# Norms of the branches: squares summed on four output strips, inverse roots spread back by products on four row strips

## The reference

```
def head_norm(o, g, center):
    of = o.astype(jnp.float32)
    if center:
        of = of - jnp.mean(of, axis=-1, keepdims=True)
    y = of * lax.rsqrt(jnp.mean(of * of, axis=-1, keepdims=True) + EPS) * g.astype(jnp.float32)
...
    br_conv = jax.nn.silu(layernorm(conv + w['conv_b'], w['conv_ln_g'], w['conv_ln_b']))
    br_ret = jax.nn.silu(r_g) * head_norm(r_o, w['ret_gn'], center=True)
    br_gla = jax.nn.silu(g_r) * head_norm(g_o, w['gla_gn'], center=False)
    br_diff = head_norm(d_o, w['diff_subln'], center=False) * (1.0 - lam_init)
    gate = jax.nn.sigmoid(gates.reshape(B, L, N_BRANCH, D_MODEL))
    merged = jnp.einsum('blnc,ncd,blnd->bld', branches, w['w_branch'], gate)
    h = h + merged @ w['w_out']
```

## Time and profile before

| | |
|---|---|
| time, median of 3 runs | 2790.89 us (2789.33 to 2792.15) |
| span of the profiled execution | 2789.1 us |
| PE busy | 2767.2 us, 99% |
| DVE busy | 1986.8 us, 71% |
| ACT busy | 1206.8 us, 43% |
| norms of the branches, layer 0 | 838.15 to 869.78 us, with two gate tiles and a late gate tile |

### The profile page before, as it was taken

The page is one execution under the profiler, slowest core; times in us unless marked ns, Lnnn a source line. Parts: engine busy times, 40 slices in busy tenths (PEclk is TensorE's granted clock), DMA queues, the critical chain, the costliest instruction groups (busy, mean ns, idle before and its releaser), DMA issues.

```text
span 2789.1 us, 57776 instructions
## 1 busy us (share of the span) xinstructions
PE 2767.2 (99%) x21828; PEld 2687.1 (96%) x21828; DVE 1986.8 (71%) x3589; ACT 1206.8 (43%) x2160; POOL 128.2 (5%) x234
## 2 busy tenths in 40 slices
PE   8999999999999999999999999999999999999999
PEld 7999999998899999999999999999888999999999
DVE  8889534478667688887488895344787676899952
ACT  6445323435435254445254453234354343544521
POOL 0000001230000000000000000012300000000000
PEclk9999999999999999999999999999999999999999
DMA  4222326463234312223212223255733343122233
GB/s 138 91 95 98 108 75 198 155 202 131 98 117 172 140 64 91 90 90 114 91 67 92 90 98 106 68 198 163 214 118 121 108 178 130 61 92 103 98 106 103
DMA packets 104815, 325.92 MB, mean 117 GB/s; under 512 B 15055, under 2 KB 31855, under 8 KB 103104
## 3 DMA queue, kind: packets, MB, share of 16 engines
q1 hardware_dynamic: 91728, 280.67, 29.2%
q0 software_dynamic: 12912, 42.86, 4.8%
HBM read 291.45 MB, written 30.94 MB: 116 GB/s over the span
## 4 chain that ended last, share of the span: by engine, by line
PE 98%; DVE 1%; ACT 1%; issue 0%; DMA 0%; DVEq 0%; ACTq 0%; POOLq 0%
PE ps L1420 52%; PE ps L1449 35%; PE ps L1626 3%; PE ps L1432 1%; PE ps L1695 1%; PE ps L1911 1%; PE ps L1747 1%; PE ps L1728 1%; PE ps L1775 0%; PE ps L1795 0%; PE ps L1677 0%; PE ps L1737 0%; PE ps L1851 0%; PE ps L1934 0%; PE ps L1777 0%
## 5 line engine op out<-in xcount | busy, mean ns | idle before, releaser
L2063 DVE TENSOR_TENSOR w_lo<-w_raw,w_hi 128x1024 fp32r<-128x1024 f32 x240 | 292.7, 1224 | 353.0 <-ACT w_hi L814 349.4
L1449 PE MATMUL ps<-x_more,w_hi 128*128 128x296 f32 (+1 forms) x2112 | 456.8, 298 | 1.2 <-DVE x_more L2927 0.8
L1449 PE MATMUL ps<-x_hi,w_hi 128*128 128x296 f32 (+1 forms) x1408 | 420.0, 298 | 1.2 <-DVE w_lo L2101 1.2
L1449 PE MATMUL ps<-x_hi,w_lo 128*128 128x296 f32 (+1 forms) x1408 | 420.4, 299 | 0.0
L1449 PE MATMUL ps<-x_lo,w_hi 128*128 128x296 f32 (+1 forms) x1408 | 420.4, 299 | 0.0
L814 ACT ACTIVATE w_hi<-w_raw 128x1024 fp32r<-128x1024 f32 x224 | 234.9, 1053 | 407.2 <-PE ps L1420 240.1
L1420 PE MATMUL ps<-x_hi,w_hi 128*128 128x296 f32 (+1 forms) x1600 | 362.4, 308 | 3.8 <-ACT hT L1162 3.8
L2101 DVE TENSOR_TENSOR w_lo<-w_raw,w_hi 128x512 fp32r<-128x512 f32 x440 | 296.6, 690 | 88.4 <-ACT w_hi L862 85.8
L1449 PEld LDWEIGHTS ps<-x_more,w_hi 128*128 128x128 f32 x2112 | 351.0, 188 | 2.4 <-issue 1.3
L1420 PE MATMUL ps<-x_hi,w_lo 128*128 128x296 f32 (+1 forms) x1600 | 347.3, 299 | 0.0
L1420 PE MATMUL ps<-x_lo,w_hi 128*128 128x296 f32 (+1 forms) x1600 | 347.2, 298 | 0.0
(11 more groups left out here) (378 smaller groups left out, 4926.9 us busy)
## 6 DMA issues: line engine op xcount, KB each, us to landing
w_raw<-wstream SPq DMA_DIRECT2D x420, 512.0 KB, 3.6
kpage<-cache_k SPq DMA_DIRECT2D x128, 128.0 KB, 3.1
vpage<-cache_v POOLq DMA_DIRECT2D x128, 128.0 KB, 3.8
gate_rows<-hT SPq DMA_DIRECT2D x48, 296.0 KB, 2.3
d_sg<-gate_rows SPq DMA_DIRECT2D x16, 888.0 KB, 5.3
h_rows<-hT SPq DMA_DIRECT2D x2, 2368.0 KB, 9.5
hT<-h_rows SPq DMA_DIRECT2D x2, 2368.0 KB, 8.7
hT<-h_in SPq DMA_DIRECT2D x4, 592.0 KB, 8.3
```

Source lines behind the costliest of these rows:

```text
L1449: mm = pe.matmul(ps[:, bank, 0:span()], wp[:, k, :], xp, start=new and k == 0 and n == 0, stop=k == KH - 1 and n == 2, skip_group_check=True)
L2063: v.tensor_tensor(w_lo[:, slot, :, :], w_raw[:, slot, :, :], w_hi[:, slot, :, :].bitcast(F32), ALU.subtract).then_inc(weights_low, 1)
```

## The change

The squares of a tile are no longer summed with a 128x128 matrix of ones. A tile is cut into four strips of 148 columns (`strip()`), and each strip is multiplied with 32 columns of ones, so that its sums land on 32 rows of PSUM: strip r on rows 32r to 32r+31 of the same bank and columns (`strip_sums`, L1450 of the changed kernel). What took 592 columns on all rows takes 148. The sums of four norms fit in two banks, so one logarithm and one exponential over 128 x 592 do for four norms, and a second group (two logarithms, one exponential over 128 x 444) for the other three. The inverse roots go back to all 128 rows by products with a fourth matrix of ones, `ones[:, 3, :]`, from 32 rows each: strip r into its own bank (`spread`, L1456). VectorE's `normed` (L2857) reads them from PSUM, four banks at once.

The orders are changed with this. The first four sums stand ahead of the means. Gate tile 22 is cut in two halves: one in front of the mean over the conv tiles, one behind the first spread. The semaphore `hn_summed` becomes `hn_spread`. Three waits are new on TensorE: for two norms done (`hn_normed`, 2) ahead of the second spread, for four ahead of the third, and for all seven ahead of the first branch product. The matrix of ones grows from 192 to 256 KB.

```diff
-        ones = keep("ones", [P, 3, P])
+        ones = keep("ones", [P, 4, P])
...
+        HEAD_NORMS = (od_tiles[0:1], od_tiles[1:2], gla_tiles[0:1], gla_tiles[1:2], ret_tiles[0:1], ret_tiles[1:2], conv_tiles)
+        FIRST_NORMS = 4
+
+        def sum_at(i):
+
+            return i % FIRST_NORMS // 2, i % 2 * strip()
+
+        FIRST_SPREAD, LAST_SPREAD = (2, 3, 4, 5), (0, 1, 2, 3)
...
                 for i in range(4):
-                    square(i, HEAD_NORMS[i][2][0][0])
+                    square(i, HEAD_NORMS[i][0][0])
                 gate_out(l, 21)
-                for i in range(4):
-                    root(i)
-                for i in range(4):
-                    inverse(i)
+                root(FIRST_NORMS, 64, split_cols(hn_root[:, 0, :]), pair(0))
+                inverse(1, 0, 4)
                 for i, tile in enumerate((2, 3, 0, 1)):
                     act.wait_ge(hn_centered, i + 1)
                     square(4 + i, branch_tiles[tile])
                 gate_activated(l, 22)
-                for i in range(4, 7):
-                    act.wait_ge(hn_normed, i - 3)
-                    root(i)
-                for i in range(4, 7):
-                    inverse(i)
+                root(6, 64, hn_root[:, 1, 0:2 * strip()], ps[:, 0, 0:2 * strip()])
+                root(7, 256, hn_root[:, 1, 2 * strip():3 * strip()], ps[:, 1, 0:strip()])
+                inverse(3, 1, 3)
...
+            def strip_sums(bank, c, mat, tile, start=True, stop=True):
+
+                n = strip()
+                for r in range(4):
+                    mm = pe.matmul(ps[32 * r:32 * r + 32, bank, c:c + n], mat, tile[:, r * n:(r + 1) * n], start=start, stop=stop)
+                return mm
+
+            def spread(banks, c, roots, n):
+
+                for r, bank in enumerate(banks):
+                    mm = pe.matmul(ps[:, bank, c:c + n], ones[32 * r:32 * r + 32, 3, :], roots[32 * r:32 * r + 32, 0:n], start=True, stop=True)
+                return mm
...
-                for j in range(2):
-                    sum_tile(j, ones[:, 1, :], branch_tiles[2 + j]).then_inc(hn_summed, 1)
+                for i in range(FIRST_NORMS):
+                    total(i)
                 pe.wait_ge(gate_tanh, 21)
                 for j in range(2):
-                    mm = sum_tile(2, ones[:, 0, :], branch_tiles[j], start=j == 0, stop=j == 1)
-                mm.then_inc(hn_summed, 1)
-                for i, (banks, width, tiles) in enumerate(HEAD_NORMS):
...
-                    if i in (3, 6):
-                        early_gates(l, 8)
+                    sum_tile(1 + j, ones[:, 1, :], branch_tiles[2 + j]).then_inc(hn_spread, 1)
+                early_gates(l, 4)
+                pe.wait_ge(root_logs, 4 + 1)
+                for j in range(2):
+                    mm = sum_tile(0, ones[:, 0, :], branch_tiles[j], start=j == 0, stop=j == 1)
+                mm.then_inc(hn_spread, 1)
+                pe.wait_ge(hn_root_ready, 1)
+                pe.wait_ge(hn_centered, 2)
+                spread(FIRST_SPREAD, 0, hn_root[:, 0, 0:2 * strip()], 2 * strip()).then_inc(hn_spread, 1)
+                early_gates(l, 4)
+                pe.wait_ge(hn_normed, 2)
+                spread(FIRST_SPREAD, 0, hn_root[:, 0, 2 * strip():4 * strip()], 2 * strip()).then_inc(hn_spread, 1)
+                pe.wait_ge(hn_centered, 4)
+                for i in range(FIRST_NORMS, len(HEAD_NORMS)):
+                    total(i)
+                early_gates(l, 8)
+                pe.wait_ge(hn_root_ready, 2)
+                pe.wait_ge(hn_normed, 4)
+                spread(LAST_SPREAD, 0, hn_root[:, 1, 0:3 * strip()], 3 * strip()).then_inc(hn_spread, 1)
...
                 def normed(i):
-                    v.wait_ge(hn_root_ready, i + 1)
-                    for tile, c in HEAD_NORMS[i][2]:
+                    v.wait_ge(hn_spread, 3 + min(i // 2, 2) + 1)
+                    banks = FIRST_SPREAD if i < FIRST_NORMS else LAST_SPREAD
+                    c0 = (i % 2 if i < FIRST_NORMS else i - FIRST_NORMS) * strip()
+                    for tile, c in HEAD_NORMS[i]:
                         gain = coef[:, 6:7] if i < 2 else prm[:, c:c + 1]
-                        ins = v.scalar_tensor_tensor(live(tile), live(tile), gain, live(hn_root[:, i % 4, :]), ALU.mult, ALU.mult)
+                        ins = v.scalar_tensor_tensor(by_strip(tile), by_strip(tile), gain, ps[:, banks[0]:banks[-1] + 1, c0:c0 + strip()], ALU.mult, ALU.mult)
```

More of the change, by code:

```diff
@@ L264, in span, with strip, by_strip @@
             return width[0]
+        def strip():
+            return span() // 2
+        def by_strip(ap):
+            return live(ap).rearrange("p (r t) -> p r t", r=4)
         def live(ap):
@@ L495, in build @@
         conv_loaded, conv_tanh, conv_gated, conv_rows, conv_done = (msem("conv_" + n) for n in ("loaded", "tanh", "gated", "rows", "done"))
-        hn_summed, hn_centered, hn_squared, hn_totalled, hn_root_ready, hn_normed = (
-            msem("head_norm_" + n) for n in ("mean", "centered", "squared", "totalled", "root", "normed"))
+        hn_spread, hn_centered, hn_squared, hn_totalled, hn_root_ready, hn_normed = (
+            msem("head_norm_" + n) for n in ("spread", "centered", "squared", "totalled", "root", "normed"))
         root_logs = msem("root_logs")
@@ L1279, in square, with root, inverse @@
                     act.activation(hn_sq[:, i % 4, :], tile, ACT.Square).then_inc(hn_squared, 1)
[L1281 to L1288, removed]
+                def root(end, width, room, sums):
+                    act.wait_ge(hn_totalled, end)
+                    act.activation(room, sums, ACT.Ln, bias=EPS, scale=1.0 / width).then_inc(root_logs, 1)
+                def inverse(end, n, count):
+                    act.wait_ge(root_logs, 4 + end)
+                    room = hn_root[:, n, 0:count * strip()]
+                    act.activation(room, room, ACT.Exp, scale=-0.5).then_inc(hn_root_ready, 1)
                 act.wait_ge(prompt_evac, 10)
@@ L1972, in head_norms, with total @@
                 live_columns(l)
-                for j in range(2):
-                    sum_tile(j, ones[:, 1, :], branch_tiles[2 + j]).then_inc(hn_summed, 1)
+                def total(i):
+                    mat = ones[:, 0, 0:32] if i == 6 else ones[:, 1, 48:80]
+                    tiles = HEAD_NORMS[i]
+                    for n in range(len(tiles)):
+                        pe.wait_ge(hn_squared, i + n + 1)
+                        mm = strip_sums(*sum_at(i), mat, hn_sq[:, (i + n) % 4, :], start=n == 0, stop=n == len(tiles) - 1)
+                    mm.then_inc(hn_totalled, 1)
@@ L1992, in gates @@
+                spread(FIRST_SPREAD, 0, hn_root[:, 0, 2 * strip():4 * strip()], 2 * strip()).then_inc(hn_spread, 1)
[6 more added lines that the diff above has]
+                spread(LAST_SPREAD, 0, hn_root[:, 1, 0:3 * strip()], 3 * strip()).then_inc(hn_spread, 1)
             def gates(l):
-                pe.wait_ge(root_logs, 4 + 7)
+                pe.wait_ge(root_logs, 4 + 3)
@@ L2004, in gates @@
                             pe.wait_ge(br_split, 2 * n + 2)
+                        if m == 0 and n == 0:
+                            pe.wait_ge(hn_normed, 7)
                         if n in (0, 3):
@@ L2796, in head_norms @@
                 v.wait_ge(conv_steps, len(taps))
-                for i, (tile, banks, width) in enumerate(((2, 0, 64), (3, 1, 64), (0, 2, 256), (1, 2, 256))):
-                    v.wait_ge(hn_summed, min(i, 2) + 1)
+                for i, (tile, banks, width) in enumerate(((2, 1, 64), (3, 2, 64), (0, 0, 256), (1, 0, 256))):
+                    v.wait_ge(hn_spread, min(i, 2) + 1)
                     x = split_cols(branch_tiles[tile])
@@ L3037, in constants @@
     block_of = [np.arange(P) // b for b in (128, 64, 32)]
-    ones = np.stack([(b[:, None] == b[None, :]) for b in block_of], axis=1).astype(f)
     row = np.arange(P)
+    spread = (row[:, None] % 8 == 0) & (row[:, None] % 32 // 8 == row[None, :] // 32)
+    ones = np.stack([(b[:, None] == b[None, :]) for b in block_of] + [spread], axis=1).astype(f)
     seq_of = 2 * np.arange(4)[None, :] + row[:, None] // 64
```

2 lines of the change are left out of this document (removed).

## The result

The changed kernel takes 2798.25 us (median of 11 runs), the kernel before 2792.15 us beside it; the ratio is **1.0025, 95% interval 1.0016 to 1.0033**. By the ratio that is 7.0 us slower (the two medians differ by 6.1). It is clear of no change, while the 0.2% that the prediction set as its bound lies inside the interval. (One execution of the changed kernel took 13882.63 us; the comparison leaves it out.)

The account below looks back on a forecast made before the run. PE, busy 99% of the span and throughout the norm stretch, was taken as the bound. 2 x (1.75 net of waits and saving + 1.7 clock) = 6.9 us slower: span 2796.0, median 2797.8, range 2791.5 to 2802.

Parts of the forecast that it names:

- the 0.2% that the prediction set as its bound: Whole kernel: a measurement tells about 0.2%, 5.6 us, from no change; slower begins at 2796.5 us.
- PE's saving: Norm stretch: strip sums and spreads replace 32 sum-of-squares records; PE's work falls 2.6 us a layer, 5.3 in all.
- The first wait: Before the second spread: PE waits 3.1 us for VectorE's two norms, whose chain ends 7.3 us after the conv mean.
- The second wait: Before the third branch product: PE waits 1.4 us for ScalarE's late gate tanh, delayed 3.7 us by VectorE's last norms.
- No third wait: Fourth branch product: VectorE's first take is ready at 876.1, PE comes at 876.4, so no wait, but just so.
- The clock: Behind PE's idle before the second spread: granted clock falls in each layer, costing 1.7 us; bounds 0 and 3.4.
- Reading the roots from PSUM: VectorE's norms: reading PSUM adds nothing to 1.54 us for two; bounds 0.1 us less and 0.3 more.
- The constants: Kernel opening: the extra 64 KB of the `ones` tile cost nothing, at most a few tenths of a microsecond.
- The rival of no wait: Norm stretch: PE never waits and keeps its whole gain, -5.3 us, 2785.6; chance 0.06.
- The sum of 6.9 us: Whole kernel: 2 x (1.75 for both waits less saved work + 1.7 for lower clock) = 6.9 us slower.

Follow-up runs that it names:

- the filled ones: Changed kernel plus five fp32 products of 296 columns, results unread, put in front of PE's wait before the second spread: ratio 1.0017 to the kernel before.
- The kernel with both edits: Changed kernel with VectorE's silu products, weight part and coefficient between second and third centering, and the last spread mid gate tile 23: 0.9987 to the kernel before.

## Why the prediction was right

- **PE's saving** was put at 2.6 us a layer. With both waits taken out it is 38.18 - 35.59 = 2.59 us in layer 0. (The 0.09 us of going into the first strip products lies ahead of the first point and is not in it.) In layer 1, with 288 columns, it is 2.20 us, and 2.5 without the 0.3 us of waiting left there. Its parts hold too: a spread of 296 columns 0.71 us, one of 444 columns 862.02 - 861.06 = 0.96, a strip group 0.251 where I had 0.253.
- **The first wait** was put at 3.1 us; it is 2.91 and 2.97. VectorE's chain from the conv mean to the second spread took 7.2 us where I had 7.3. Two edits moved the wait as the sum says: taking about 4 us out of the chain (845.18 to 849.25) removed it, and two blocks moved past the mean shortened it by 1.6.
- **The second wait** was put at 1.4 us; it is 1.24 and 1.48. It goes when the last spread stands four blocks earlier, but for 0.24 us in layer 1, so its cause is that spread and VectorE's and ScalarE's chain behind it, as said.
- **No third wait** at the fourth branch product: right.
- **The clock** was put at 1.7 us a layer, on the ground that idling uses the array still less than small products do. It fell behind 7 of 8 such waits, for 1.7 us each, and behind none of the filled ones. This was the least certain term. By the profiles it is right in its size and nearly always right in its coming; had it not come, the sum would have been 3.5 us and "no change that can be told". The ground given for it does not carry it alone: waits of 2.28 and 2.33 us, which use the array as little while they last, left the clock at its full level. And the choice of 1.7 over 3.4 us was a choice between two rows, not a derivation.
- **Reading the roots from PSUM** was taken as free: two norms take 1.57 us, and took 1.57 to 1.58 before.
- **The constants**: PE's first wait is 11.4 and 11.7 us in the two profiles of the changed kernel and 11.3 and 11.2 in those of the kernel before, a few tenths at most; the steady products of the first phase begin at 37.75 in the first profile of the one and 37.90 in that of the other. No price shows, as taken; tenths of a microsecond could hide in the spread of that wait.
- **The rival of no wait** was put at -5.3 us and called the most that this change can gain. The kernel with both edits is that rival made real, but for the 0.3 us left in layer 1: its stretches are 2.59 and 2.20 us shorter, 4.8 in all, and its total 3.6 us lower with an interval of 1.1 to 6.1.
- The sum of 6.9 us met a measured 7.0. Part of that closeness is luck: the runs of one kernel spread over some 6 us by falls of the clock outside the stage.

## What to carry to other kernels

When an engine at 99% gets less work, look at whose results its new waits need, and add up that engine's in-order queue behind the last thing it was given: here 5.3 us of products saved were worth less than the waits, and the clock behind them, that came with one mean moved four gate blocks later and the last norms started later. Move the helper's independent work into the gap that the new order opens, and only there: the same move that repaired the changed kernel cost the old one 0.2%. Time a stage by two fixed points of the timeline when the effect is smaller than the noise of the whole run.

## What the runs showed of the hardware that I had not expected

- Products on four output strips run fully side by side in fp32: 0.251 us for four of 148 columns. Four products from 32 rows each run side by side too, with 0.21 us on top of what one alone streams, whether they have 296 or 444 columns.
- The granted clock falls in this kernel without any idle time, in the retention and GLA stages, where groups of small products (such as 32 records of 64x8 in 1.1 us) stand between gate products, and differently from run to run: 5.1 and 8.6 us lost in the two profiles of one and the same kernel, none in one profile of the kernel with products in the wait. The executions of one kernel spread over 5.9 us (before) and 6.1 us (changed), nearly as much as the whole effect studied here.
- A wait of PE costs more than the idle that the profile lists for it: taking out one of 1.24 us saved 1.47, in part because the first pair of products behind it takes 0.34 us where 0.27 is the pace.
- A wait of 2.97 us once left the clock at its full 2.4 GHz, where the same wait had halved it in three other profiles of that layer. A wait of 2.3 us did not bring it down in either layer of its profile, one of 1.3 to 1.4 us neither.
